# A Trainium2 block kernel with the operands and the work area placed 64 bytes higher in SBUF

## The reference, cut to what matters

```python
def swiglu(h, w13, w2):
    g, u = jnp.split(h @ w13, 2, axis=-1)
    return (jax.nn.silu(g) * u) @ w2
...
        x = x + y
        x = x + swiglu(rmsnorm(x, norm_ffn_g[i]), f_w13[i], f_w2[i])
```

## Time and profile before

| | |
|---|---|
| Median of 3 runs | 1972.4 us |
| The three runs | 1970.05, 1972.4, 1981.9 us |
| The profiled execution, own time | 1969.42 us |
| Its span, first to last instruction | 1967.6 us |
| TensorE busy, matmuls / weight loads | 1894.0 us (96%) / 1729.2 us (88%) |
| VectorE busy | 1375.0 us (70%) |
| ScalarE busy | 921.0 us (47%) |
| GpSimd busy | 46.4 us (2%) |
| DMA queue of SyncE | 364.58 MB, 54.9% of 16 engines' span |
| Mean granted TensorE clock | 0.991 of full speed |

### The profile page before, as it was taken

One profiled execution on the slowest core, in us unless ns is written; L12 is line 12 of the kernel. 1 busy time (PEld: TensorE's weight loads), 2 busy tenths in 40 slices (PEclk: granted clock), 3 DMA queues, 4 the chain that ended last, 5 costly groups with the idle time before them and its releaser, 6 DMA issues.

```text
span 1967.6 us, 32453 instructions
## 1 busy us (share of the span) xinstructions
PE 1894.0 (96%) x13360; PEld 1729.2 (88%) x13360; DVE 1375.0 (70%) x1577; ACT 921.0 (47%) x991; POOL 46.4 (2%) x65
## 2 busy tenths in 40 slices
PE   6999998899999979999999999999989999999999
PEld 6998888788888769999989899987879999999998
DVE  4777977766777666666667666678997666676665
ACT  4544745555666553433345453334334333444332
POOL 0000000000000000001101000000000000000000
PEclk8999999999999989999999999999999999999999
DMA  6553343786788747555554385552324555555553
GB/s 216 175 172 101 127 144 150 262 307 265 287 303 306 255 141 195 186 192 192 192 171 130 108 254 193 191 190 88 108 82 154 188 192 193 176 193 172 192 192 107
DMA packets 243771, 365.97 MB, mean 186 GB/s; under 512 B 12550, under 2 KB 217817, under 8 KB 231257
## 3 DMA queue, kind: packets, MB, share of 16 engines
q1 hardware_dynamic: 243673, 364.58, 54.9%
HBM read 363.50 MB, written 1.05 MB: 185 GB/s over the span
## 4 chain that ended last, share of the span: by engine, by line
PE 83%; DVE 10%; ACT 2%; issue 2%; DMA 2%; SPq 1%; POOL 0%; DVEq 0%; ACTq 0%
PE proj L960 40%; PE proj L1522 11%; PE acc L1294 11%; PE proj L979 7%; PE acc L1486 5%; DVE ring_lo L2506 2%; ACT ring_hi L1935 1%; PE acc L1307 1%; DMA raw<-in_w_in_dram 1%; PE proj L1789 1%; PE acc L1004 1%; PE proj L1628 1%; PE misc L1467 0%; PE acc L1586 0%; PE acc L1111 0%
## 5 line engine op out<-in xcount | busy, mean ns | idle before, releaser
L2506 DVE TENSOR_TENSOR ring_lo<-raw,ring_hi 128x2048 fp32r<-128x2048 f32 x242 | 560.0, 2317 | 213.5 <-ACT ring_hi L1935 212.3
L1935 ACT ACTIVATE ring_hi<-raw 128x2048 fp32r<-128x2048 f32 x242 | 462.3, 1914 | 441.6 <-PE proj L960 205.9
L960 PE MATMUL proj<-h_hi,ring_hi 128*128 128x256 f32 x1424 | 407.3, 286 | 10.2 <-DVE ring_lo L2506 10.0
L960 PE MATMUL proj<-h_lo,ring_hi 128*128 128x256 f32 x1424 | 396.0, 278 | 0.0
L960 PE MATMUL proj<-h_hi,ring_lo 128*128 128x256 f32 x1424 | 395.9, 278 | 0.0
L960 PE MATMUL proj<-g_hi,ring_hi 128*128 128x256 f32 x1088 | 303.0, 279 | 1.2 <-DVE g_lo L2550 1.2
L960 PE MATMUL proj<-g_lo,ring_hi 128*128 128x256 f32 x1088 | 301.8, 277 | 0.0
L960 PE MATMUL proj<-g_hi,ring_lo 128*128 128x256 f32 x1088 | 301.8, 277 | 0.0
L960 PEld LDWEIGHTS proj<-h_hi,ring_hi 128*128 128x128 f32 x1424 | 268.3, 188 | 21.9 <-DVE ring_lo L2506 11.2
L960 PEld LDWEIGHTS proj<-h_lo,ring_hi 128*128 128x128 f32 x1424 | 269.3, 189 | 3.8 <-issue 2.9
L960 PEld LDWEIGHTS proj<-h_hi,ring_lo 128*128 128x128 f32 x1424 | 268.4, 189 | 0.0
(11 more groups left out here) (451 smaller groups left out, 3423.7 us busy)
## 6 DMA issues: line engine op xcount, KB each, us to landing
raw<-in_f_w_dram SPq DMA_DIRECT2D x132, 1024.0 KB, 5.0
raw<-in_w_in_dram SPq DMA_DIRECT2D x29, 1024.0 KB, 5.4
raw<-in_w_exp_gate_dram SPq DMA_DIRECT2D x25, 1024.0 KB, 5.0
raw<-in_w_exp_up_dram SPq DMA_DIRECT2D x24, 1024.0 KB, 4.8
raw<-in_a_w_in_dram SPq DMA_DIRECT2D x24, 1024.0 KB, 5.1
raw<-in_w_exp_down_dram SPq DMA_DIRECT2D x23, 1024.0 KB, 5.9
raw<-in_b_w_qkv_dram SPq DMA_DIRECT2D x12, 1024.0 KB, 5.1
raw<-in_c_w_in_dram SPq DMA_DIRECT2D x12, 1024.0 KB, 5.1
```

Source lines behind the costliest of these rows:

```text
L960: last = pe.matmul(bank[:, a, :], w[:, k, a * P:(a + 1) * P], h[:, k, :], start=(k == 0 and w is hi and h is h_h and (a == 0 or not first) ...
L1935: act.activation(w_hi[n.slot][:, :], raw[n.slot][:, :], ACT.Copy).then_inc(hi_ready, 1)
L2506: dve.tensor_tensor(w_lo[n.slot][:, :], raw[n.slot][:, :], w_hi[n.slot][:, :].bitcast(f32), SUB)\
```

## The change

One unused tile of 64 bytes, `fill`, is allocated between `eps_col` and `h_hi`, and the start of the work area is rounded up to a multiple of 128 rather than of 32. `h_hi`, `h_lo`, `ident`, `ones`, `params` and `inv_b` and every tile of the work area move up by 64 bytes: `h_hi` from 98,624 to 98,688 (771 x 128), `work0` from 118,592 to 118,656 (927 x 128). The load buffers, the ring, `x_res` and the five small tiles stay. No instruction is added, removed or reordered.

```diff
         neg_half = sb("neg_half", [P, 16])
         eps_col = sb("eps_col", [P, 1])
+        sb("fill", [P, 16])
         h_hi = sb("h_hi", [P, KT, SEQ], f32r)
...
-        work0 = -(-nc.sbuf_base // 32) * 32
+        work0 = -(-nc.sbuf_base // 128) * 128
         limit = nc.sbuf_usable_end - work0
```

## The result

The changed kernel takes 2010.0 us (median of four runs, 2009.4 to 2013.6) against 1973.4 us for four runs of the kernel before: a ratio of 1.0182, interval 1.0160 to 1.0205. It is 36.6 us slower. The prediction said 1971 us, no change, and gave a slowdown of over 1% a chance of 5%; the time lies outside its range.

A forecast was written before the change was run, and what follows sets the result against it. TensorE was taken as the bound, with a matmul in flight for 96% of the span. All terms were 0, added to the profiled 1969.4 us; with the runs' scatter the forecast was 1971 us, range 1964 to 1982.

The forecast's parts named there:

- Both together: Matmuls whose two operands now both lie on multiples of 128: taken as 0, range -8.1 to +11.4 us.
- Moving operand: Matmuls moving `h` or `g` (64 off) against line 979 moving the aligned ring: 277 to 279 ns, so 0.
- Stationary operand: Weight loads of the aligned ring (189 ns) against the 64-off `h_lo` (188 ns): 0.
- ScalarE, VectorE: Their chunk reads and writes at either placement: 1906 against 1908 ns, and 2290 against 2290, so 0.
- DMA and small tiles: Loads into moved tiles: 0, range -0.3 to +7 us; work-area tiles not ending on multiples of 128: 0.
- slower by the matmul's pace: Feed-forward rounds and a fast piece of 528 settle at 117.8 ns: 19.8 us more, 1991 us; chance 4%.

The follow-up runs named there:

- The sweep: Separate kernels of matmul blocks with the operands' distance varied modulo 256 or 512 bytes; at 512 columns, 227.9 ns at 0, 229.1 at 64, 233.3 at 192.
- e1: Against the kernel before, everything 64 bytes higher, the ring too, so operands have the changed kernel's addresses at the old distance: 1972.95 us, ratio 1.0004.
- e7: Against the kernel before, load buffers, ring and residual 192 bytes higher, operands and work area unmoved, distance as in the changed kernel: 2009.05 us, ratio 1.0182.
- e10: Against the kernel before, `h` and work area at distance 112 modulo 256 from the ring, feed-forward hidden tiles at distance 0: 1973.23 us, ratio 0.9991.
- e3: Against the kernel before, only the work area 64 bytes higher, `h` and the other tiles unmoved: 1995.9 us, ratio 1.0134.
- e6: Separate kernel of matmul blocks: finer distance steps, line 979's order, 512 columns, longer pauses; 112 gives 113.7 ns, 4 bytes less 120.0, 4 more 121.7.
- e5: Separate kernel, only matmuls within a block, moving operand offset 0 to 496 bytes: 119.9 ns at 0, 117.8 at 64, 117.8 then 113.5 at 192.
- e8: Separate kernel of matmul blocks with one pair of tiles at another distance, unrounded operands, or 128 columns: unrounded 215.8 ns at 0, 64, 112 and 192.

## Why the prediction was wrong

**The step that failed is "Both together".** It named the relation of the two operands as the only thing that the rows could not show, and then priced it at 0, with +11.4 us as the upper end. The whole change of +37 us is this term.

- *Its price came from the wrong rows.* The rows used are 512 columns wide, and their two placements differ by 1 ns. The sweep shows that at 512 columns the effect has another order and is smaller beside the matmul (227.9 ns at distance 0, 229 to 235 elsewhere). I carried 1.0 ns over to 256 columns by width; there it is 5.1 to 5.3 ns in line 960. The upper end was no bound: an unshown relation had been bounded by rows of a different shape.
- *Its control group was none.* The pairs of the earlier trace rows set "moved 64 off" beside "moved aligned". But both pairs of tiles stand unlike, one at distance 192, the other at 64. Their equal means fit that place does not matter, which e1 shows, and say nothing about being alike. Equal numbers from two cases that share the property in question are no evidence on it.
- *"Moving operand" and "Stationary operand": right.* 0 each, as far as place goes (e1, e7).
- *ScalarE, VectorE: right.* 1906 to 1908 and 2290 ns before, 1909 to 1913 and 2290 to 2291 now.
- *DMA and small tiles: right in the time, thin in the rows.* The changed profile lists `raw_spare` loads at 6.6, 6.3 and 5.1 us and aligned `raw` at 6.3, 4.9 and 6.5 for the same sources; e10, with `raw_spare` moved too, has 5.6, 5.0 and 4.9, as before. What settles it is e1, where `raw_spare` has the very address of the changed kernel and its loads take 5.8, 5.1 and 4.8 us, and e7, where it kept its old address and they take 6.5, 5.2 and 5.1. In these profiles the loads are longer where the matmuls are slower, not where `raw_spare` moved, and TensorE's steps leave nothing over for them. So the Trainium skill's rule on 256-byte cuts (page "DMA: Bandwidth & Descriptors", section "How a descriptor splits into AXI transactions"), from which the prediction worked out 7 us, made no difference that these runs show.
- *The rival "slower by the matmul's pace"* was nearest: it named the term, its size per matmul (4.2 ns) and the point of decision, 11.3 us for a piece of 96. 11.51 was measured. Its reason was wrong: it let the placement choose between the two paces of before, which was worth 19.8 us. Distance 0 has a pace of its own, 120.0 ns, to which the slow pieces of before fall too; 3,888 matmuls at 6.5 ns are 25 us and 1,104 at 2.2 ns another 2.4, and the mixers' pieces and line 979, which the rival did not count, are most of the rest. The 3.5 us that it added for the down products did not come: they are 1.5 us faster. 4% was too little for a rival whose mechanism was marked as not understood and lay on the largest term.

What the runs do not settle: why 0 is slow and 112 and 192 are fast, and what chooses 113.5 or 117.8 ns at 192 (e3 points to the products ahead, e6 shows no effect of a longer pause). At 64, which has 117.8 ns in every block of e5 and e6, the kernel before also has 113.3 for 77 matmuls of line 979 in a row, within the first piece of the earlier trace rows. And 192 of the experts' down products read the second set, which stands at distance 0 from `hid` before and after, yet their mean step falls from 230.7 to 226.8 ns; there the distance does not give the pace by itself, and no run isolates what else does. The cause of the slowdown does not hang on these: e1, e7 and e5 show it, and at distance 0 the 256-wide products of lines 960 and 979 had one pace wherever it was measured.

## What to carry to other kernels

Where TensorE is the bound and its operands are rounded fp32, the start addresses of the two operands belong to the tuning, by their difference modulo 256 bytes, separately for each width; "all on the same multiple" was among the slowest choices at 256 columns and the best at 512. Before moving tiles, list for each large group of matmuls that difference before and after, and price a difference that the trace does not hold as unknown, not as zero. An edit that inserts a small tile ahead of others can move the time by 2%, as it did here, so a comparison of two kernels has to look at this first.

## What the runs showed of the hardware

- A matmul of rounded fp32 operands, 128 x 128 weights and 256 columns, takes 113.5 to 122.1 ns from start to start at full granted clock (e5, e6). The distance of its operands modulo 256 bytes fixes the pace of these blocks at 0 (119.9 ns) and 112 (113.8); at 192 there are two, 113.5 and 117.8, and what chooses is open. 512 columns take 227 to 235 ns (e5, e6), and unrounded fp32 of 256 columns 215.8 at every distance tried (e8).
- The Trainium skill, page "SBUF — State Buffer", section "Who interferes with whom", says that TensorE reads the moving operand and the weights through two independent ports and never waits on anyone. The traces agree that no other engine matters (e5 has the paces of 0, 64 and 192 with none at work), but the two reads do not look independent: the pace depends on how their addresses stand to each other.
- The Trainium skill, page "TensorE: Matmul & The Clock Gate", section "Wait — 56ns, not 53.3ns?", gives a start-to-start time of the columns by 2.4 GHz and some 2.5 ns. From this sum 256 columns would take 109.2 ns, an estimate; for 512 the page has 215.7. Rounded operands never reach it here, with some 113.5 and 227 ns at best. Unrounded operands of 256 columns take 215.8 ns, the page's figure for twice the columns; no run here shows why.
